# Three-pass chunk states and stacked sample updates in the retention, and a reordered last group before the final projection, in a two-layer retention and Mamba-2 step

## The reference, cut to what matters

```python
def step(s, inp):                       # chunked_linear_recurrence, one chunk
    qc, kc, vc, lac = inp
    cum = jnp.cumsum(lac, axis=1)
    ...
    scores = jnp.einsum('bihd,bjhd->bhij', qc, kc) * decay
    intra = jnp.einsum('bhij,bjhe->bihe', scores, vc)
    cross = jnp.einsum('bihd,bhde->bihe', qc, s) * jnp.exp(cum)[..., None]
    tail = jnp.exp(cum[:, -1:, :] - cum)
    s_new = jnp.exp(cum[:, -1, :])[..., None, None] * s + jnp.einsum('bjhd,bjh,bjhe->bhde', kc, tail, vc)
    return s_new, intra + cross

# retention_layer: 4 heads, keys of 256, values of 512
o, s_new = chunked_linear_recurrence(q, k, v, log_a, s0)
o = (_rms(o).reshape(b, L, RET_VW) * head_norm).astype(h.dtype)
return (o * jax.nn.silu(gate)) @ w_out, s_new
# ssd_layer_full: 32 heads in 8 groups, states of 128 x 64
g = _rms((y * jax.nn.silu(z)).reshape(b, L, SSM_GROUPS, -1)) * gate_norm
return g @ w_out, s_new, new_conv
```

## Time and profile before

| what | value |
|---|---|
| median of three runs | 2116.76 us (2107.05 to 2120.87) |
| profiled execution, its own time | 2116.82 us |
| its span | 2115.0 us |
| PE busy | 2006.0 us, 95% |
| DVE busy | 1305.3 us, 62% |
| ACT busy | 909.6 us, 43% |
| POOL busy | 382.0 us, 18% |

### The profile page before, as it was taken

One profiled execution on the slowest core, in us unless ns is written; L12 is line 12 of the kernel. 1 busy time (PEld: TensorE's weight loads), 2 busy tenths in 40 slices (PEclk: granted clock), 3 DMA queues, 4 the chain that ended last, 5 costly groups with the idle time before them and its releaser, 6 DMA issues. The chain is left out here.

```text
span 2115.0 us, 40755 instructions
## 1 busy us (share of the span) xinstructions
PE 2006.0 (95%) x14006; PEld 1836.3 (87%) x14006; DVE 1305.3 (62%) x1961; ACT 909.6 (43%) x2011; POOL 382.0 (18%) x552
## 2 busy tenths in 40 slices
PE   6999999999899998999899999999999999968998
PEld 6999999999778776788788999999999999946887
DVE  7755899866365567323234768685868677756422
ACT  6321212232344455223244656555555555475331
POOL 0200000000122221000000434342434433430000
PEclk9999999999999998999999999999999999978999
DMA  4433333332688899244432333233333333384431
GB/s 136 133 100 107 89 108 99 109 102 82 207 286 280 263 303 311 85 125 144 147 81 56 81 95 93 75 99 83 91 88 99 97 81 89 77 256 141 122 122 40
DMA packets 386922, 274.10 MB, mean 130 GB/s; under 512 B 117672, under 2 KB 342664, under 8 KB 386664
## 3 DMA queue, kind: packets, MB, share of 16 engines
q1 hardware_dynamic: 339968, 243.48, 39.2%
q10 hardware_dynamic: 46752, 28.06, 4.4%
HBM read 184.59 MB, written 86.88 MB: 128 GB/s over the span
## 5 line engine op out<-in xcount | busy, mean ns | idle before, releaser
L1607 PE MATMUL p3acc_ps<-xn2hi,p3whi 128*128 128x272 f32 x1536 | 460.7, 300 | 6.8 <-ACT p3mid L1812 3.7
L1607 PE MATMUL p3acc_ps<-xn2lo,p3whi 128*128 128x272 f32 x1536 | 445.4, 290 | 0.0
L1607 PE MATMUL p3acc_ps<-xn2hi,p3wlo 128*128 128x272 f32 x1536 | 445.2, 290 | 0.0
L270 PE MATMUL p1ps<-x1hi,w1hi 128*128 128x272 f32 x1288 | 372.9, 290 | 3.1 <-issue 2.6
L270 PE MATMUL p1ps<-x1hi,w1lo 128*128 128x272 f32 x1288 | 372.6, 289 | 0.0
L270 PE MATMUL p1ps<-x1lo,w1hi 128*128 128x272 f32 x1288 | 371.7, 289 | 0.0
L1607 PEld LDWEIGHTS p3acc_ps<-xn2hi,p3whi 128*128 128x128 f32 x1536 | 292.1, 190 | 15.4 <-issue 15.2
L1607 PEld LDWEIGHTS p3acc_ps<-xn2lo,p3whi 128*128 128x128 f32 x1536 | 292.5, 190 | 0.0
L1607 PEld LDWEIGHTS p3acc_ps<-xn2hi,p3wlo 128*128 128x128 f32 x1536 | 291.8, 190 | 0.0
L270 PEld LDWEIGHTS p1ps<-x1hi,w1hi 128*128 128x128 f32 x1288 | 243.2, 189 | 3.5 <-issue 3.5
L270 PEld LDWEIGHTS p1ps<-x1hi,w1lo 128*128 128x128 f32 x1288 | 243.6, 189 | 0.0
(11 more groups left out here) (332 smaller groups left out, 4281.0 us busy)
## 6 DMA issues: line engine op xcount, KB each, us to landing
w1raw<-in_ret_w_in SPq DMA_DIRECT2D x48, 512.0 KB, 5.0
p3raw<-in_ssm_w_in SPq DMA_DIRECT2D x48, 512.0 KB, 4.6
ret_vg<-y1out SPq DMA_DIRECT2D x32, 512.0 KB, 3.2
r_vg<-ret_vg SPq DMA_DIRECT2D x32, 512.0 KB, 5.3
r_sin<-in_state_ret SPq DMA_DIRECT2D x32, 512.0 KB, 6.3
out_ret_sample<-r_sout ACTq DMA_DIRECT2D x32, 512.0 KB, 6.7
s_cr<-sums SPq DMA_DIRECT2D x64, 256.0 KB, 3.4
ret_qk<-y1out SPq DMA_DIRECT2D x16, 512.0 KB, 3.7
```

What stands on the lines that cost most here:

```text
L270: last = nc.tensor.matmul(bank[:, 2 * at + i, 0:HB], w[s][:, idx, k, :], x[:, idx, k, i * HB:(i + 1) * HB], start=(k == 0 and j == 0), sto ...
L1607: last = nc.tensor.matmul(pr_ps[:, n % 2, 0:TB], wt[:, j % 2, k, :], x[:, k, b * TB:(b + 1) * TB], start=(k == 0 and i == 0), stop=(k == K ...
```

## The change

It has three parts. In the retention the sample update is stacked: for each half of the eight sequences (u = 0, 1) the partitions hold the values as hi, lo, hi and zeros (`vst`) and the keys as hi, hi, lo and zeros (`kst`), so that one product of 128 partitions gives all three terms. The samples' keys and values are loaded once, not twice, and turned to 64 rows. Second, the chunk's state product is made in three float32r passes on halves (`kt_hi`, `kt_lo`, `v_hi`, `v_lo`, in one buffer each). Third, in the last SSD group the weights come two blocks per chunk, p4's first tile is loaded at c = 3, the roots run at c = 7, `sample_state(g, 0)` moves ahead on VectorE, and p4's first tile takes its passes as the halves come.

```diff
+        kst = sb(ctx, "r_kst", [P, 2, RDK], F32R)
+        vst = sb(ctx, "r_vst", [P, 2, RDV], F32R)
+        quarters = [slice(i * NS // 2, (i + 1) * NS // 2) for i in range(4)]
+        v_hi, v_lo = spare[:, 1, 0:RDV], spare[:, 1, RDV:2 * RDV]
+        kt_hi, kt_lo = spare[:, 0, 0:RDK], spare[:, 0, RDK:2 * RDK]
...
 # TensorE, sample(x)
-                        nc.tensor.matmul(sb_ps[:, k, :], ktm[:, x % 2, cols], vhi[:, :], start=True, stop=False)
-                        last = nc.tensor.matmul(sb_ps[:, k, :], ktm[:, x % 2, cols], vlo[:, :], start=False, stop=True)
+                        last = nc.tensor.matmul(sb_ps[:, k, :], ktm[:, x % 2, cols], vst[:, 2 * c // NCH, :], start=True, stop=True)
 # TensorE, states(t)
+                    pe.wait_ge(c_low, t + 1)
                     wait(pe, st_add, t)
                     for k in range(NK):
-                        last = nc.tensor.matmul(st_ps[:, k, :], kt[:, t % 2, k * P:(k + 1) * P], v[:, t % 2, :],
-                                                start=True, stop=True)
+                        cols = slice(k * P, (k + 1) * P)
+                        for i, (keys, values) in enumerate(((kt_hi, v_hi), (kt_hi, v_lo), (kt_lo, v_hi))):
+                            last = nc.tensor.matmul(st_ps[:, k, :], keys[:, cols], values, start=(i == 0), stop=(i == 2))
 # ScalarE
+                def chunk_highs(t):
+                    act.wait_ge(k_ev, chunk_turn(t) + 1)
+                    wait(act, st_mm, t)
+                    nc.scalar.activation(v_hi, v[:, t % 2, :], ACT.Copy)
+                    nc.scalar.activation(kt_hi, kt[:, t % 2, :], ACT.Copy).then_inc(c_high, 1)
                 def samples_by_tokens(h):
-                    nc.scalar.activation(vs, v_ps[0:NS, :], ACT.Copy)
-                    nc.scalar.activation(vhi[:, :], v_ps[:, :], ACT.Copy).then_inc(v_ev, 1)
+                    nc.scalar.activation(vs, v_ps[0:NS, :], ACT.Copy).then_inc(v_ev, 1)
...
+                def sample_keys_high(h):
+                    act.wait_ge(k_ev, samples_turn(h) + 1)
+                    for u in range(2):
+                        for rows in (quarters[u], quarters[2 + u]):
+                            last = nc.scalar.activation(kst[rows, u, :], vs_ktf[quarters[2 + u], 0:RDK], ACT.Copy)
+                    last.then_inc(k_high, 1)
 # ScalarE, step t
                     if c == 1:
-                        own(t - 1)
+                        sample_keys_high(h)
                     if t:
                         state_high(t - 1)
+                    if c == 1:
+                        own(t - 1)
...
                     if t >= 2:
                         store_sample(t - 2)
+                    if following:
+                        chunk_highs(t + 1)
                     square(chunk_y(t), P)
 # VectorE
+                def chunk_lows(t):
+                    dve.wait_ge(c_high, t + 1)
+                    nc.vector.tensor_tensor(v_lo, v[:, t % 2, :], v_hi, ALU.subtract)
+                    nc.vector.tensor_tensor(kt_lo, kt[:, t % 2, :], kt_hi, ALU.subtract).then_inc(c_low, 1)
+                def sample_values(h):
+                    dve.wait_ge(v_ev, samples_turn(h) + 1)
+                    for u in range(2):
+                        for rows in quarters[0:2]:
+                            last = nc.vector.tensor_copy(vst[rows, u, :], vs_ktf[quarters[u], :])
+                    last.then_inc(v_high, 1)
+                    dve.wait_ge(v_high, h + 1)
+                    for u, rows in enumerate(quarters[0:2]):
+                        last = nc.vector.tensor_tensor(vst[quarters[2 + u], u, :], vs[rows, :], vst[rows, u, :], ALU.subtract)
+                    last.then_inc(halves, 1)
+                def sample_keys_low(h):
+                    dve.wait_ge(k_high, h + 1)
...
 # VectorE, step t
                     if t >= 2:
                         sample_state(t - 2)
                     if c == 1 and h:
                         gate_samples(h - 1)
+                    if c == 1:
+                        sample_values(h)
                     if t:
                         state_low(t - 1)
+                    if c == 1:
+                        sample_keys_low(h)
+                    if following:
+                        chunk_lows(t + 1)
                     if c:
                         next_state(t)
...
                         decay_scores(samples_turn(h), h, scs[:, :], P, NS)
-                        sample_halves(h)
 # SSD layer, last group: SP, ScalarE, VectorE
-                            for k in range(3 * c, min(3 * c + 3, KI)):
-                                weights.load(sp, k)
-                            if c == NCH - 3:
+                            if c == 3:
...
                                 next_tile.load(sp)
+                            for k in range(2 * c, 2 * c + 2):
+                                weights.load(sp, k)
...
-                            if c == NCH - 2:
+                            if c <= KI - LATE4:
+                                weights.high(act, c - 1)
+                            else:
                                 next_tile.roots(act)
-                            else:
-                                weights.high(act, c - 1 if c < NCH - 2 else c - 2)
...
-                        if c == 1 and more:
+                        if c == 1:
                             sample_state(g, 0)
...
-                        if c == 1 and not more:
-                            sample_state(g, 0)
 # p4, first tile: TensorE
+                def products_as_halves_come(i):
+                    part_ks = range(KP * i, KP * (i + 1))
+                    pe.wait_ge(hi_done, part(0, i))
+                    for k in part_ks:
+                        pe.wait_ge(weights.high_done, k + 1)
+                        one_pass(0, k, ghi, whi, k == 0, False)
+                    pe.wait_ge(lo_done, part(0, i))
+                    for k in part_ks:
+                        one_pass(0, k, glo, whi, False, False)
+                    for k in part_ks:
+                        pe.wait_ge(weights.low_done, k + 1)
+                        last = one_pass(0, k, ghi, wlo, False, k == KI - 1)
```

102 lines of the change are left out of this document (54 added, 48 removed).

## The result

The changed kernel took 2121.09 us (median of 20 runs) against 2114.54 for the kernel before in as many: ratio 1.0027, 95% interval 1.0017 to 1.0038. It is 0.3% slower; 1% faster was forecast.

The account below looks back on a forecast made before the run. TensorE, busy for 95% of the span, was taken as the bound, with a sample-state loop binding next in the retention. Retention -13 and last group with p4's start -10 gave -23 us from 2116.82: 2094 us, range 2079 to 2111.

Parts of the forecast that it names:

- The sample steps: Retention, c = 0 and c = 1: scores' gain and VectorE's added work cancel; 0, between -5.6 and +10 us.
- The loop of a sample state: Retention, heads 0 to 2: load, halves, update and next load bind at 7.15 us a step; -14.5 us.
- The last group: Last SSD group: `p4ri` issued two chunks earlier and read one later, so ScalarE's wait goes; -8.0 us.
- p4's start: p4's first tile: TensorE starts with the first activations' high half, 1912.45 instead of 1914.45; -2.0 us.
- TensorE's 0.80 us a step: Retention: sample update saves 0.46 us, state product 0.34; a step of 7.56 becomes 6.76 if TensorE alone paces.
- The named sign of error: Prediction wrong if VectorE's sample work at c = 1 holds TensorE for more than 2 us.
- Start and last head: Retention: the start waits for first halves, +1.5 us; the last head, bound by VectorE, 0, from -4 to +6.
- blocks 14 and 15 are covered: Last group: these weight blocks, issued at c = 7, are needed only after eight other roundings in p4.
- the transfers hold the retention: Rival, chance 0.20: landing goes to 7.3 us, retention steps stay at 7.56; 2105 us in total.

Follow-up runs that it names:

- decay_first: Changed kernel with VectorE's decay of the next chunk's scores ahead of the gate; ratio 1.0022 to the kernel before.
- thin_stores: mended plus decay_first's order, each new sample state stored with 32 KB instead of 512 KB; ratio 0.9886 to the kernel before.
- thin_stores_before: Kernel before, with each new sample state stored with 32 KB instead of 512 KB; ratio 0.9981 to the kernel before.
- ahead_but_sample_step: mended with the chunk halves ahead of the state halves on ScalarE and VectorE, except in the sample step; 2100.62 us, ratio 0.9935 to the kernel before.
- own_behind: Changed kernel with ScalarE's masked sample keys behind the sums and the next chunk's halves in the sample step; ratio 0.9983 to the kernel before.
- weights_by_three: Changed kernel with the last group's weight loads three to a chunk, as before the change; ratio 1.0013 to the kernel before.
- mended: Changed kernel with own_behind, weights_by_three and the next head's sample loads behind the state's load; 2104.99 us, ratio 0.9952 to the kernel before.
- last_group_only: Kernel before with only the change's last SSD group and p4's first tile, retention unchanged; ratio 0.9981 to the kernel before.

## Why the prediction was wrong

23 us faster were forecast, and the kernel came out 6.5 slower. By the table, one profile each, most of that lies in the retention: 10.7 us longer between the first and the last state update, where 14.5 less were forecast. The sample steps grew by 51.1 - 41.9 = 9.2 us, for a term of 0. The other steps of heads 0 to 2, which carry most of the loop's -14.5, grew by 164.8 - 163.0 = 1.8. The last group and p4's start gave 14.5 - 9.5 = 5.0 us of their 10. Term by term:

- **TensorE's 0.80 us a step**: right where TensorE waits for nothing. decay_first has steps of 6.78 us and thin_stores a mean of 6.81, against 6.76. In the changed kernel such a step takes 7.03, since TensorE waits for VectorE's decay; the working put this wait at nothing, because VectorE's sum (5.86) lay below 6.76.
- **The loop of a sample state**, -14.5 us in three heads: the mechanism is right, its price is the other step that failed. The landing was 6.7 us in the median, as taken, and with the halves behind the state the loop is the bound (thin_stores, thin_stores_before). But the prediction spread a late landing evenly, 7.15 us a step. A step is 7.03 or, when a state is late, 8.8 to 9.1: the halves and the decay queue behind it, and TensorE pays up to 1.4 us at once. The middle steps gave 1.0 us in place of at least 6. With the halves ahead of the state they gave 114.8 - 108.0 = 6.8 (ahead_but_sample_step). It also missed SyncE's loads of samples ahead of a state, 2.9 us in a loop that had no slack left. The turn grew by 3.5 us and is longer in every kernel with the passes (24 to 29 us; 21 to 23 without); no run took that apart.
- **The sample steps**, "0, between -5.6 and +10": the step that failed first. +9.2 us lies within the bounds by luck, since the reason is not among those that were priced. The working summed VectorE's operations and let 1.4 us reach TensorE. It did not follow ScalarE's order, where `own` waits for VectorE and has the sums and the next chunk's highs behind it. The named sign of error, VectorE's sample work holding TensorE for more than 2 us, came true with 2.37 us. VectorE's copies were priced too high: in the view of this tile they take 0.42 us at the least and 0.45 in the median, not 0.69. That is the prediction's estimate of 0.42 by the Trainium skill, "VectorE: DVE Perf Modes", section "Mode 2×_2P — use both read ports for one tensor", and the trace agrees. Each part alone leaves these steps as they were, within what the clock does to them (42.4 and 44.2 us; 41.9 and 46.9 without either); both together make them 51.1, and own_behind gives 9 us back.
- **The clock** was no term at all. Behind the wait in the sample step it fell to 0.50 in head 1, and the step behind took 2.2 us more in heads 0 and 1 than in head 2.
- **Start and last head**: +2.0 for +1.5, and 66.6 to 67.3 us for 0; right.
- **The last group**, -8.0: 6.7 us came, the wait for `p4ri` is gone. But "blocks 14 and 15 are covered" looked at who needs the blocks, not at what stands behind them in SyncE's queue: the last sample store, 2.8 us. weights_by_three shows it.
- **p4's start**, -2.0: right as far as the working went. TensorE starts with the first `p4ghi`, and VectorE's low halves end at 1944.55, 22.3 us after it, as computed (22.0), without TensorE waiting for them. One of the 2.0 us is lost behind the first tile, where ScalarE's copy of the stacked sums stands behind a wait for a load (0.96 us at TensorE): the same kind of step, which the working did not follow that far.

Of the rivals, "the transfers hold the retention" was nearest in kind, but it has 2105 us and steps of 7.56; mended comes out at that time with middle steps of 7.3. With the order put right the change gives 0.65% (ahead_but_sample_step), where 1.1% was forecast. Slower than before needed the meeting of two queues, which no rival had.

## What to carry to other kernels

When two parts of a change put work on the same in-order engine, walk that engine's list at the one step where both stand, and ask of every instruction that waits what of the other part is queued behind it; sums of durations can't show it. Work that needs no transfer goes ahead of work that may wait for one, on every engine between, but step by step: here the same order gained in the middle steps and lost in the sample step. And when the busiest engine is relieved, look for the next bound by making it cheaper (thin stores), before and after.

## What the runs showed of the hardware

VectorE's subtraction of 128x256 with both operands in SBUF (`kt_lo`) took 0.42 us in 17 of the 31 steps from 563 us on, and 0.95 to 0.97 in 14. In all 14 GpSimd's sum of squares had begun 0.07 to 0.25 us before it, in all 17 it began later. One pair of the 14 (late step above, VectorE at 737.44) and one of the 17, GpSimd and VectorE:

```profile
737.20 0.92 POOL L1186 TENSOR_TENSOR r_sq<-r_sq 128x256 f32<-128x256 f32 x1 [5.51 <-ACT r_sq L1098]
...
744.67 0.42 DVE L1237 TENSOR_TENSOR w2hi<-r_kt,w2hi 128x256 fp32r<-128x256 f32 x1
745.96 0.74 POOL L1186 TENSOR_TENSOR r_sq<-r_sq 128x256 f32<-128x256 f32 x1 [6.56 <-ACT r_sq L1098]
```

The Trainium skill, "SBUF — State Buffer", section "Who interferes with whom", says that a VectorE instruction with two SBUF inputs contends with a GpSimd instruction that reads SBUF, and that the order of issue decides which of them is held up; the trace agrees.

The same wait of 2.3 to 2.4 us in the sample step was followed by a granted clock of 0.56 and 0.50 (stretches of 5 us) in heads 0 and 1, and of 1.00 in head 2. In before's unchanged code, too, the clock fell in some sample steps of heads 1 to 3 and not in others (before and last_group_only). What decides there was not followed up.
